# Split first products with one-hot keys from ScalarE in the experts, and GpSimd taking two steps of the picks

## The chip, the cores and the metric

The kernel runs on one NeuronCore of a Trainium2 chip. The metric is the device time of one execution in microseconds. Before the change, three runs gave a median of 3827.49 us (3822.95 to 3830.51). Engines are called TensorE (PE, its weight loads PEld), VectorE (DVE), ScalarE (ACT), GpSimd (POOL) and SyncE (SP, which here only issues DMAs).

## The reference, cut to what matters

Two transformer blocks for 512 tokens of width 1024, in float32. The change touches only the last layer of the second block, a retrieval of single-neuron experts:

```python
def peer(h, w_q, subkeys, u, v):                 # h (512, 1024)
    q = (xc @ w_q).reshape(C, 8, 2, 128)         # 8 heads, 2 halves
    s = einsum('chpd,hpnd->chpn', q, subkeys)    # scores of 2 x 128 keys a head
    sv, si = top_k(s, 16)
    cand    = sv[:, :, 0, :, None] + sv[:, :, 1, None, :]
    cand_id = si[:, :, 0, :, None] * 128 + si[:, :, 1, None, :]
    best, pos = top_k(cand.reshape(C, 8, 256), 16)
    ids = take_along_axis(cand_id.reshape(C, 8, 256), pos)   # 8 x 16 of 16384 experts
    g = softmax(best)
    a = gelu(einsum('cd,chkd->chk', xc, u[ids]))
    return einsum('chk,chkd->cd', g * a, v[ids])
```

## The kernel before, in words

**Picks** (`QueryPicks.run`). For each of 8 heads ScalarE rounds the head's weights (128x2048) to their high part, VectorE subtracts it to get the low part (`lower`, L1884), and TensorE makes 48 products (high x high, high x low, low x high; lines 110 to 112) and 8 score products. ScalarE copies the scores (L1865). VectorE then does the rest of a head: the 16 largest of each half (`top16`), the sums of candidates, the 16 largest of these, the places of the picks in the two lists (`places`), and two look-ups (`look_up`): a one-hot by comparison (L1927), its product with the indices (L1931), and a sum (L1935), each over 128x1024 elements. `keep` and `weigh` store ids and weights. `lower(h + 1)` stands ahead of head h on VectorE.

**Experts** (`peer_experts`). The 512 tokens are dealt with in two ways at once, all engines sharing both:

- The first 256 tokens gather. 512 "rows" (2 tiles of tokens x (u, v) x 128 picks) are fetched by GpSimd with an indirect DMA, 128 lines of 4 KB each (L2075), into a ring of 8 buffers. VectorE uses each in order: for u a product with the tokens and a sum (L2222), for v a multiply and add (L2229). `dealt` fixes how many rows belong to a step: 32 in the lead-in, then 480 over 128 steps, so 3 or 4 a step. A fetch waits until the row 8 earlier is used.
- The last 256 tokens are dense: all 16384 experts in 128 steps of 128. In a step TensorE makes the first products `up` (u tile x tokens, 8 products of 256 columns, L2113), the `gates` of a group of 8 tokens (L2102), and the second products `down` of the step before (L2122). ScalarE takes the GELU (L2169), VectorE multiplies it with the gates to `w` (L2259).
- The gates spread a token's 128 weights over the 16384 experts, a quarter (32 x 128) at a time. For a group, VectorE writes one-hot keys of the second index (`one_hot`, 128x1024, L2184) and of the first (`one_hot_first`, L2196), GpSimd multiplies the latter with the weights' two parts (`weighed`, L2061), TensorE multiplies both, and ScalarE (L2150) and VectorE (L2206) take the result. 32 groups are built in a lead-in ahead of the first step, one more in each of the first 96 steps, none in the last 32.

SyncE loads the u and v tile of each step (0.5 MB each, three buffers of each). The order on each engine is the order of the code; semaphores alone join them. After the experts, `turn` adds the result back into xT, the residual kept in SBUF.

## Time and profile before

| | |
|---|---|
| median of 3 runs | 3827.49 us |
| profiled execution: its time, its span | 3820.54 us, 3818.7 us |
| busy: TensorE, VectorE, ScalarE, GpSimd | 3250.4, 2243.2, 890.2, 996.6 us |
| picks | 2377 to 2627 us |
| lead-in of the experts | 2627 to 2763 us |
| 96 steps with gates | 2763 to 3545 us |
| 32 steps without | 3545 to 3780 us |
| read from HBM | 596.92 MB, over two thirds of it in the experts |

Stages are told from the first and last starts of lines in the trace. Busy times overlap. A matmul's recorded duration is longer than the distance to the next, since they are pipelined: the distance between starts is what one costs. The DMA share is the mean busy share of the 16 queues' engines.

### The profile page before, as it was taken

Reading aid. Unit: us, or ns where it says so; the run is one execution under the profiler, and the core shown is the slowest. Engines: PE = TensorE matmul, PEld = TensorE weight load, DVE = VectorE, ACT = ScalarE, POOL = GpSimd, SP = SyncE. Lnnn points to the kernel's source line nnn. Section 1 sums busy time; section 2 is a strip of 40 time slices with the busy share of each in tenths; the row PEclk is TensorE's granted clock in tenths of the full one; section 3 lists DMA queues with packets and bytes.
Section 4 is the critical chain, followed back from the end, with each engine's and each line's share of the span. In section 5 each row is a group of like instructions: output and inputs, shape, how many; then the busy total and the mean of one; then the engine's idle time right before and its main releaser. Section 6 shows DMA issues by size and latency. Waiting matters only on the chain. (4 is left out here: it accounts for less than half of the span.)

```text
span 3818.7 us, 39393 instructions
## 1 busy us (share of the span) xinstructions
PE 3250.4 (85%) x14052; PEld 2353.1 (62%) x14052; DVE 2243.2 (59%) x3986; ACT 890.2 (23%) x1354; POOL 996.6 (26%) x757
## 2 busy tenths in 40 slices
PE   6779889997968979999498897653599999999997
PEld 4645668875834658878286645443466666666664
DVE  3136433365315643356463434898988999888766
ACT  2133333312214333321324333210100000000001
POOL 0020100000002100000001200003788788888653
PEclk9868999998976989999698878875599999999999
DMA  3320022352330013243134101103499999999996
GB/s 125 132 82 1 28 72 94 108 190 100 136 108 20 1 55 99 94 150 142 63 128 119 31 4 67 51 27 109 141 338 368 373 375 375 367 369 372 401 409 251
DMA packets 206528, 618.01 MB, mean 162 GB/s; under 512 B 31472, under 2 KB 65040, under 8 KB 200720
## 3 DMA queue, kind: packets, MB, share of 16 engines
q1 hardware_dynamic: 132624, 347.28, 25.9%
q0 software_dynamic: 73728, 268.47, 18.9%
q8 instruction: 100, 1.64, 0.2%
q14 instruction: 76, 0.62, 0.1%
HBM read 596.92 MB, written 18.74 MB: 161 GB/s over the span
## 5 line engine op out<-in xcount | busy, mean ns | idle before, releaser
L110 PE MATMUL psum<-sbuf 128*128 128x512 f32 (+1 forms) x1680 | 674.5, 401 | 196.2 <-DVE sbuf L1884 98.9
L111 PE MATMUL psum<-sbuf 128*128 128x512 f32 (+1 forms) x1680 | 660.9, 393 | 0.0
L112 PE MATMUL psum<-sbuf 128*128 128x512 f32 (+1 forms) x1680 | 660.0, 393 | 0.0
L110 PEld LDWEIGHTS psum<-sbuf 128*128 128x128 f32 x1680 | 323.1, 192 | 273.8 <-DVE sbuf L1884 100.8
L2122 PE MATMUL psum<-sbuf 128*128 128x512 f32 x1024 | 469.4, 601 | 5.8 <-DVE sbuf L2259 5.8
L1206 POOL TENSOR_TENSOR sbuf<-sbuf 64x768 fp32r<-64x768 f32 (+2 forms) x22 | 29.2, 1329 | 1689.4 <-ACT sbuf L1152 1689.4
L2113 PE MATMUL psum<-sbuf 128*128 128x256 f32 x2048 | 465.8, 381 | 0.0
L2113 PEld LDWEIGHTS psum<-sbuf 128*128 128x128 f32 x2048 | 391.0, 191 | 107.3 <-issue 60.3
L2075 POOL DMA_INDIRECT sbuf<-peer_u,sbuf x256 | 383.7, 1499 | 96.5 <-issue 55.6
L2075 POOL DMA_INDIRECT sbuf<-peer_v,sbuf x256 | 328.3, 1282 | 154.6 <-DVE sbuf L2229 102.4
L111 PEld LDWEIGHTS psum<-sbuf 128*128 128x128 f32 x1680 | 323.2, 192 | 70.1 <-issue 5.0
L112 PEld LDWEIGHTS psum<-sbuf 128*128 128x128 f32 x1680 | 322.4, 192 | 67.2
L2229 DVE SCALAR_TENSOR_TENSOR sbuf<-sbuf 128x1024 f32<-128x1024 f32 x252 | 313.1, 1281 | 55.8 <-DMA sbuf<-peer_v,sbuf 54.9
L2222 DVE CUSTOM_DVE_ANT_0 sbuf<-sbuf 128x1024 f32<-128x1024 f32 x256 | 326.8, 1322 | 6.6 <-DMA sbuf<-peer_u,sbuf 6.6
L2122 PEld LDWEIGHTS psum<-sbuf 128*128 128x128 f32 x1024 | 186.4, 190 | 195.3 <-issue 183.7
L425 DVE TENSOR_TENSOR sbuf<-sbuf 128x1024 fp32r<-128x1024 f32 x88 | 107.8, 1226 | 298.3 <-ACT sbuf L421 298.3
L2102 PE MATMUL psum<-sbuf 128*128 128x64 f32 x1024 | 166.7, 312 | 92.4 <-DVE sbuf L2184 65.3
L2169 ACT ACTIVATE sbuf<-psum 128x256 f32<-128x256 f32 x128 | 49.1, 383 | 834.0 <-PE psum L2113 834.0
L2102 PEld LDWEIGHTS psum<-sbuf 128*128 128x128 f32 x1024 | 152.6, 225 | 120.7 <-DVE sbuf L2184 80.3
L2184 DVE TENSOR_TENSOR sbuf<-sbuf 128x1024 fp32r<-128x1024 f32 x128 | 195.8, 1529 | 0.0
L964 PE MATMUL psum<-sbuf 128*65 128x512 f32 (+4 forms) x384 | 184.5, 570 | 6.6 <-ACT sbuf L1166 6.3
L1038 DVE TENSOR_REDUCE sbuf<-psum 128x1 f32<-128x128 f32 (+1 forms) x192 | 106.3, 555 | 129.8 <-PE psum L896 82.3
(272 smaller groups left out, 4515.4 us busy)
## 6 DMA issues: line engine op xcount, KB each, us to landing
sbuf<-peer_ut SPq DMA_DIRECT2D x128, 512.0 KB, 8.9
sbuf<-peer_v SPq DMA_DIRECT2D x128, 512.0 KB, 6.7
sbuf<-w_ffn SPq DMA_DIRECT2D x88, 512.0 KB, 3.4
sbuf<-w_mod SPq DMA_DIRECT2D x24, 1024.0 KB, 5.0
sbuf<-w_down SPq DMA_DIRECT2D x16, 1408.0 KB, 6.1
sbuf<-w_fm SPq DMA_DIRECT2D x38, 512.0 KB, 4.4
sbuf<-w_out SPq DMA_DIRECT2D x24, 512.0 KB, 3.5
sbuf<-w_tm SPq DMA_DIRECT2D x10, 1024.0 KB, 5.8
```

What stands on the lines that cost most here:

```text
L110: nc.tensor.matmul(acc, w_high(k), x_high(k), start=(k == 0), stop=False)
L111: nc.tensor.matmul(acc, w_high(k), x_low(k), start=False, stop=False)
L112: mm = nc.tensor.matmul(acc, w_low(k), x_high(k), start=False, stop=(k == kt - 1))
L425: self.nc.vector.tensor_tensor(self.w_low[:, j, :], self.w[:, j, :], self.w_high[:, j, :].bitcast(F32), ALU.subtract).then_inc(self.low_do ...
L964: mm = nc.tensor.matmul(summed[0:W, i % SUMS, x.q0[j]:S], v[0:x.kw[j], x.v, j, :], prob[0:x.kw[j], i % 2, j, x.q0[j]:S], start=(j == 0), s ...
L2075: pool.indirect_dma_start(rows[:, n % RING, :], None, (u, v)[f], bass.IndirectOffsetOnAxis(ap=stream[:, t, j:j + 1], axis=0)).then_inc(gat ...
L2102: mm = nc.tensor.matmul(g_ps[:, n % 2, 2 * j * QUARTER:2 * (j + 1) * QUARTER], hot[:, n % 2, j, :], part[:, n % 2, j, :, :], start=True, s ...
L2113: mm = nc.tensor.matmul(a_ps[:, s % 2, 0:DENSE], u_in[:, s % HELD, k * P:(k + 1) * P], hT[:, k, tok0:S], start=(k == 0), stop=(k == KT - 1))
L2122: mm = nc.tensor.matmul(y_ps[:, 2 * t + half, :], w[:, s % 3, t * P:(t + 1) * P], v_in[:, s % HELD, half * S:(half + 1) * S], start=(s == ...
L2184: nc.vector.tensor_tensor(hot[:, n % 2, :, :], C.iota[:, :].unsqueeze(1).to_broadcast([P, GROUP, NKEY]), picked[:, 1, toks].unsqueeze(2).t ...
L2222: nc.vector.tensor_tensor_reduce(out=rows[:, r, :], in0=rows[:, r, :], in1=h_tok[:, t, :], scale=1.0, scalar=0.0, op0=ALU.mult, op1=ALU.ad ...
L2229: nc.vector.scalar_tensor_tensor(sums, rows[:, r, :], dots[:, t, j:j + 1], sums, ALU.mult, ALU.add).then_inc(used[r], 1)
```

## The change

In `peer_experts`:
- `up` is split in the same three products as the projections (`split_products`), with ScalarE making the high part of each u tile and VectorE the low part, two steps ahead. The tokens' high and low parts are made once, at the start.
- The one-hot keys of the second index go to ScalarE in all groups of the steps and in every other group of the lead-in: (key - index) squared, then ReLU(1 - that).
- To make room, the ring of row buffers lies in xT and hT. xT is stored to HBM at the start of the stage and read back near its end.
- `weighed` runs one group further ahead of the fetches on GpSimd, and u tiles are loaded behind v tiles on SyncE.

In `QueryPicks.run`, GpSimd takes `lower` and the products of the look-ups. `find`, `keep` and `weigh` of a head move into the next head's code.

```diff
@@ picks, VectorE
-                lower(0)
                 for h in range(PH):
-                    if h + 1 < PH:
-                        lower(h + 1)
                     dve.wait_ge(copied, 2 * h + 2)
                     top16([(sc[:, h % 2, p, t, :], sc2[:, p, t, :], val[:, p, t, :], idx[:, p, t, :])
                            for p in range(2) for t in range(ST)])
...
-                    places()
-                    dve.wait_ge(topped, h + 1)
                     if h == 0:
                         dve.wait_ge(iota_landed, 16)
-                    look_up(0)
-                    look_up(1)
-                    keep(h)
-                    if h:
+                    else:
+                        find(h - 1)
+                        keep(h - 1)
                         weigh(h - 1)
+                    places(h)
+                    compare(h)
+                find(PH - 1)
+                keep(PH - 1)
                 weigh(PH - 1)
+
+            @block.gpsimd
+            def _(pool):
+                def lower(h):
+                    pool.wait_ge(high_done, h + 1)
+                    nc.gpsimd.tensor_tensor(w_low[:, h % 2, :], w[:, h % 2, :], w_high[:, h % 2, :].bitcast(F32),
+                                            ALU.subtract).then_inc(low_done, 1)
+
+                lower(0)
+                lower(1)
+                for h in range(PH):
+                    pool.wait_ge(topped, h + 1)
+                    for p in range(2):
+                        n = 2 * h + p
+                        pool.wait_ge(compared, n + 1)
+                        if h:
+                            pool.wait_ge(summed, n - 1)
+                        nc.gpsimd.tensor_tensor(hot2[:, p, :, :].rearrange("p (t k) a -> p t k a", t=ST),
+                                                hot[:, p, :, :].rearrange("p (t k) a -> p t k a", t=ST),
+                                                idf[:, h % 2, p, :, :].unsqueeze(2).to_broadcast([P, ST, T, T]), ALU.mult
+                                                ).then_inc(looked, 1)
+                    if h + 2 < PH:
+                        lower(h + 2)
@@ experts
+    rows = [(xT, hT)[r // 4][:, r % 4 * 2:r % 4 * 2 + 2, :].rearrange("p k s -> p (k s)") for r in range(RING)]
+    def on_act(n):
+        return n >= GROUPS or n % 2 == 1
@@ SyncE
+            sp.dma_start(x_d, xT[:, :, :].rearrange("p k s -> p (k s)")).then_inc(x_stored, 16)
...
+            for n in range(ROWS - RING, ROWS - RING // 2):
+                wait_row(sp, n)
+            sp.dma_start(xT[:, :, :].rearrange("p k s -> p (k s)"), x_d).then_inc(x_back, 16)
@@ GpSimd
                     if n >= RING:
                         wait_row(pool, n - RING)
+                    elif n < RING // 2:
+                        pool.wait_ge(x_stored, 16)
+                    else:
+                        pool.wait_ge(h_low_made, 1)
...
+            weighed(0)
             for step in range(-GROUPS, NKEY):
-                if step + GROUPS < QUARTERS * GROUPS:
-                    weighed(step + GROUPS)
+                if step + GROUPS + 1 < QUARTERS * GROUPS:
+                    weighed(step + GROUPS + 1)
                 fetch_rows(step)
@@ TensorE
-                pe.wait_ge(u_landed[s % HELD], 16 * (s // HELD + 1))
-                for k in range(KT):
-                    mm = nc.tensor.matmul(a_ps[:, s % 2, 0:DENSE], u_in[:, s % HELD, k * P:(k + 1) * P], hT[:, k, tok0:S],
-                                          start=(k == 0), stop=(k == KT - 1))
-                mm.then_inc(a_made, 1)
+                pe.wait_ge(u_low_made, s + 1)
+                split_products(nc, a_ps[:, s % 2, 0:DENSE], KT, lambda k: u_high[:, s % 2, k * P:(k + 1) * P],
+                               lambda k: u_low[:, s % 2, k * P:(k + 1) * P], lambda k: h_high[:, k, :],
+                               lambda k: h_low[:, k, :]).then_inc(a_made, 1)
@@ ScalarE
+            def split_u(s):
+                act.wait_ge(u_landed[s % HELD], 16 * (s // HELD + 1))
+                nc.scalar.activation(u_high[:, s % 2, :], u_in[:, s % HELD, :], ACT.Copy).then_inc(u_high_made, 1)
+            def one_hot(n):
+                if n >= 2:
+                    act.wait_ge(gates_made, n - 1)
+                for j in range(GROUP):
+                    at = n % GROUPS * GROUP + j
+                    nc.scalar.activation(hot[:, n % 2, j, :], C.iota[:, :], ACT.Square, bias=picked[:, 1, at:at + 1],
+                                         scale=-1.0).then_inc(squared, 1)
+                act.wait_ge(squared, GROUP * (squares(n) + 1))
+                nc.scalar.activation(hot[:, n % 2, :, :], hot[:, n % 2, :, :].bitcast(F32), ACT.Relu, bias=C.ones[:, 0:1],
+                                     scale=-1.0).then_inc(one_made, 1)
@@ VectorE
+            def split_u(s):
+                dve.wait_ge(u_high_made, s + 1)
+                if s >= 2:
+                    dve.wait_ge(a_made, s - 1)
+                nc.vector.tensor_tensor(u_low[:, s % 2, :], u_in[:, s % HELD, :], u_high[:, s % 2, :].bitcast(F32),
+                                        ALU.subtract).then_inc(u_low_made, 1)
```

The order of instructions, at three places. First VectorE in the picks, from the places of a head on; before:

```order
L1923 TENSOR_TENSOR sbuf<-sbuf 128x64
L1927 TENSOR_TENSOR sbuf<-sbuf 128x1024
L1931 TENSOR_TENSOR sbuf<-sbuf 128x1024
L1935 TENSOR_REDUCE sbuf<-sbuf 128x64
L1927 TENSOR_TENSOR sbuf<-sbuf 128x1024
L1931 TENSOR_TENSOR sbuf<-sbuf 128x1024
L1935 TENSOR_REDUCE sbuf<-sbuf 128x64
```

The same place now, up to the next head's first search (L1885):

```order
L1919 TENSOR_TENSOR sbuf<-sbuf 128x64
L1927 TENSOR_TENSOR sbuf<-sbuf 128x1024 x2
L1885 MAX sbuf<-sbuf 128x8 x8
L1888 MAX_INDEX sbuf<-sbuf 128x8
L1889 MATCH_REPLACE sbuf<-sbuf 128x128
```

The multiplies left for GpSimd, and the sums come a head later. This is GpSimd's order in the picks now (it had no work there before): L1988 is `lower`, L2000 the two multiplies of a head.

```order
L1988 TENSOR_TENSOR sbuf548<-sbuf533,sbuf547 128x2048 x2
L2000 TENSOR_TENSOR sbuf567<-sbuf566,sbuf555 128x1024 x2
L1988 TENSOR_TENSOR sbuf548<-sbuf533,sbuf547 128x2048
L2000 TENSOR_TENSOR sbuf567<-sbuf566,sbuf555 128x1024 x2
L1988 TENSOR_TENSOR sbuf548<-sbuf533,sbuf547 128x2048
```

The subtract for head h+2 stands behind the multiplies of head h. Last, ScalarE in one dense step with gates, before (L2169 the GELU, L2150 the take of the gates):

```order
L2169 ACTIVATE sbuf<-psum 128x256
L2150 ACTIVATE sbuf<-psum 128x32x8
L2169 ACTIVATE sbuf<-psum 128x256
L2150 ACTIVATE sbuf<-psum 128x32x8
L2169 ACTIVATE sbuf<-psum 128x256
```

and now (L2255 the GELU, L2210 the high part of u, L2229 the take, L2218 and L2221 the one-hot keys):

```order
L2255 ACTIVATE sbuf<-psum 128x256
L2210 ACTIVATE sbuf<-sbuf 128x1024
L2229 ACTIVATE sbuf<-psum 128x32x8
L2218 ACTIVATE sbuf<-sbuf 128x128 x8
L2221 ACTIVATE sbuf<-sbuf 128x1024
```

Ten instructions join the two of a step, and the keys of the next group are written ahead of the next GELU.

## Rows read from the trace of the kernel before

**Rows 1.** Windows by stage: busy time of each engine, clock, DMA share.

```profile
core 0: us, PE busy (x) PEld busy (x) DVE busy (x) ACT busy (x) POOL busy (x), PEclk, DMA share, GB/s
2377.00:2627.00 250.00, 119.93 (x512) 96.87 (x512) 227.09 (x982) 38.55 (x54) 0.00 (x0) 0.74 0.09 30
2627.00:2763.00 136.00, 65.89 (x277) 60.63 (x277) 123.53 (x177) 13.29 (x34) 98.84 (x72) 0.50 0.53 168
2763.00:3545.00 782.00, 758.46 (x3063) 518.45 (x3063) 673.25 (x970) 75.89 (x196) 629.57 (x455) 1.00 0.97 366
3550.00:3750.00 200.00, 195.17 (x674) 127.02 (x672) 136.84 (x130) 11.12 (x29) 115.90 (x102) 1.00 1.03 408
```

**Rows 2.** Waits of VectorE, 2763 to 3545, then 3545 to 3800 (total, times, longest).

```profile
DVE sbuf L2259 <- ACT sbuf L2169: 107.9, 73, 4.6
...
DVE sbuf L2229 <- DMA sbuf<-peer_v,sbuf: 54.9, 63, 1.5
```

**Rows 3.** Timeline of TensorE, one step with gates (start, duration).

```profile
3351.42 3.62 PE L2113 MATMUL psum<-sbuf 128*128 128x256 f32 x16
3354.69 1.16 PE L2102 MATMUL psum<-sbuf 128*128 128x64 f32 x8
3355.68 3.68 PE L2122 MATMUL psum<-sbuf 128*128 128x512 f32 x8
3359.20 0.38 PE L2113 MATMUL psum<-sbuf 128*128 128x256 f32 x1
```

**Rows 4.** Timeline of TensorE, split products of 256 columns in a projection.

```profile
2015.05 0.28 PE L111 MATMUL psum<-sbuf 128*128 128x256 f32 x1
...
2015.89 0.28 PE L112 MATMUL psum<-sbuf 128*128 128x256 f32 x1
```

**Rows 5.** Timeline of the next one-hot; line L2184 in all (minimum, median, maximum).

```profile
3359.36 1.22 POOL L2061 TENSOR_TENSOR sbuf<-sbuf 128x512 fp32r<-128x512 f32 x1
3359.60 2.06 DVE L2184 TENSOR_TENSOR sbuf<-sbuf 128x1024 fp32r<-128x1024 f32 x1
3360.74 1.78 POOL L2075 DMA_INDIRECT sbuf<-peer_u,sbuf  x1 [0.15 <-issue]
3362.82 0.94 POOL L2075 DMA_INDIRECT sbuf<-peer_u,sbuf  x1 [0.30 <-issue]
...
L2184 DVE TENSOR_TENSOR sbuf<-sbuf x128: 1210/1220/2072, 2634.3 to 3539.6; 128x1024 fp32r<-128x1024 f32 x128
```

**Rows 6.** ScalarE lines L2160 and L421 (minimum, median, maximum, ns).

```profile
L2160 ACT ACTIVATE sbuf<-sbuf x2: 309/309/309, 2978.0 to 3532.6; 128x128 f32<-128x128 f32 x2
...
L421 ACT ACTIVATE sbuf<-sbuf x88: 1052/1060/1061, 511.9 to 1663.7; 128x1024 fp32r<-128x1024 f32 x88
```

**Rows 7.** Groups of GpSimd, 2763 to 3545 (busy, mean ns, idle before).

```profile
L2075 POOL DMA_INDIRECT sbuf<-peer_u,sbuf x218 | 322.0, 1477 | 90.0 <-issue 53.0 <-DVE sbuf L2222 35.6 <-DVE sbuf L2229 0.7
L2075 POOL DMA_INDIRECT sbuf<-peer_v,sbuf x141 | 196.3, 1392 | 60.8 <-issue 29.4 <-DVE sbuf L2229 24.3 <-DVE sbuf L2222 5.2
L2061 POOL TENSOR_TENSOR sbuf<-sbuf 128x512 fp32r<-128x512 f32 x96 | 113.9, 1187 | 2.4 <-DVE sbuf L2196 0.8
```

**Rows 8.** Picks: timeline of one head, and group L1931 of 2387 to 2600.

```profile
2451.86 1.23 DVE L1927 TENSOR_TENSOR sbuf<-sbuf 128x1024 f32<-128x1024 f32 x1
...
2460.29 2.28 DVE L1884 TENSOR_TENSOR sbuf<-sbuf 128x2048 fp32r<-128x2048 f32 x1
...
2479.29 1.09 ACT L1865 ACTIVATE sbuf<-psum 128x512 f32<-128x512 f32 x2 [2.14 <-PE psum L1835]
2479.95 1.22 DVE L1927 TENSOR_TENSOR sbuf<-sbuf 128x1024 f32<-128x1024 f32 x1
...
L1931 DVE TENSOR_TENSOR sbuf<-sbuf 128x1024 f32<-128x1024 f32 x14 | 17.2, 1226 | 0.5
```

**Rows 9.** Groups, 2637 to 2763 (the lead-in).

```profile
L2222 DVE CUSTOM_DVE_ANT_0 sbuf<-sbuf 128x1024 f32<-128x1024 f32 x32 | 64.1, 2004 | 6.6 <-DMA sbuf<-peer_u,sbuf 6.6
L2075 POOL DMA_INDIRECT sbuf<-peer_u,sbuf x38 | 61.7, 1623 | 6.6 <-issue 2.6
```

**Rows 10.** Timeline of the end of the experts.

```profile
3775.16 0.42 DVE L2259 TENSOR_TENSOR sbuf<-sbuf 128x256 f32<-128x256 f32 x1
...
3782.95 8.20 PE L1754 MATMUL psum<-sbuf 128*128 128x128 f32 x32 [3.61 <-PEq L2015]
```

More of the change, by code:

```diff
@@ L1803, in run @@
                                        "topped", "was_shifted", "exp_done", "did_step")]
+            compared, looked, summed = [sem.one(x) for x in ("compared", "looked_up", "found_summed")]
             block = ctx.enter_context(nc.Block())
@@ L1938, in keep, with find @@
+                def find(h):
+                    for p in range(2):
+                        dve.wait_ge(looked, 2 * h + p + 1)
+                        nc.vector.tensor_reduce(found[:, p, :], hot2[:, p, :, :], AX_X, ALU.add).then_inc(summed, 1)
+                    dve.wait_ge(summed, 2 * h + 2)
                 def keep(h):
@@ L1987, with peer_experts @@
 GROUP = 8
-def peer_experts(nc, C, hT, h_tok, stream, ids, weights, ut, u, v, u_in, y):
+def peer_experts(nc, C, xT, hT, h_tok, stream, ids, weights, ut, u, v, u_in, y, x_d):
     DENSE = (ST - GT) * P
@@ L2009, in dealt, with squares @@
         return EARLY + (ROWS - EARLY) * (step + 1) // NKEY
+    def on_act(n):
+        return n >= GROUPS or n % 2 == 1
+    def squares(n):
+        return sum(map(on_act, range(n)))
     def row(n):
@@ L2043, in _, with load_u @@
         def _(sp):
+            def load_u(s):
+                if s >= HELD:
+                    sp.wait_ge(u_low_made, s - HELD + 1)
+                sp.dma_start(u_in[:, s % HELD, :], ut[s]).then_inc(u_landed[s % HELD], 16)
+            sp.dma_start(x_d, xT[:, :, :].rearrange("p k s -> p (k s)")).then_inc(x_stored, 16)
+            for s in range(HELD):
+                load_u(s)
             for s in range(NKEY):
-                if s >= HELD:
-                    sp.wait_ge(a_made, s - HELD + 1)
-                sp.dma_start(u_in[:, s % HELD, :], ut[s]).then_inc(u_landed[s % HELD], 16)
                 if s >= HELD:
@@ L2096, in gates @@
             def gates(n):
-                pe.wait_ge(hot_made, n + 1)
+                if on_act(n):
+                    pe.wait_ge(one_made, squares(n) + 1)
+                else:
+                    pe.wait_ge(own_made, n - squares(n) + 1)
                 pe.wait_ge(parts_made, n + 1)
@@ L2221, in use_row @@
                 if f == 0:
-                    nc.vector.tensor_tensor_reduce(out=rows[:, r, :], in0=rows[:, r, :], in1=h_tok[:, t, :], scale=1.0,
+                    nc.vector.tensor_tensor_reduce(out=rows[r], in0=rows[r], in1=h_tok[:, t, :], scale=1.0,
                                                    scalar=0.0, op0=ALU.mult, op1=ALU.add,
```

89 lines of the change are left out of this document (57 added, 32 removed).

## The prediction

> **What bounds the kernel now.** Read the windows by stage first [rows 1]. Four stages matter. In the picks (2377 to 2627 us) VectorE is busy 227 of 250 us and GpSimd not at all. In the lead-in of the experts (to 2763) VectorE is busy 123.5 of 136 us at the low clock level of TensorE (0.50). In the first 96 dense steps (2763 to 3545, 782 us or 8.15 us a step) TensorE is busy 97%, with the DMA queues at 366 GB/s. In the last 32 steps, which have no gates to build, the queues move 408 GB/s.
>
> Then the waits [rows 2]. In the 96 steps VectorE never waits for a gathered row, only for ScalarE's GELU, which means for TensorE. In the last 32 steps it waits 54.9 us for rows. So the 96 steps are bound by TensorE, and the last 32 by transfers.
>
> The timeline of one step [rows 3] shows what TensorE does in 7.78 us (3351.42 to 3359.20): 3.27 us to the gates, 1.0 us of gates, 3.5 us of second products. The mean of 8.15 is 0.37 us more; I put it down to gates that wait for VectorE's one-hot keys.
>
> **The first products of the experts.** Eight 4-byte products of 256 columns, two passes each (16 records), become 24 single-pass products. The trace has just that shape: the split products of 256 columns in the projections start 0.12 us apart (seven intervals from 2015.05 to 2015.89 [rows 4]). 24 x 0.12 = 2.88 us for 3.27 us, so 0.39 us less. The one-hot wait of 0.37 us goes too, since ScalarE makes the keys ahead. TensorE would allow 7.39 us a step.
>
> **What the others allow.** VectorE loses the one-hot of 128x1024 (L2184) and gains the low part of u, the same shape and the same two inputs in SBUF: a swap. Its busy time stays 673/96 = 7.0 us a step. It may be blocked the same way as now: beside GpSimd's multiply the one-hot took 2.06 us for 1.22 [rows 5].
>
> ScalarE gains, per step, eight squares of 128x128 (0.31 us each as the GELU of that size, 2.5 in all), a ReLU and a copy of 128x1024 (1.06 each), beside its two present operations of 0.38: 5.4 us [rows 6]. Two ends for the squares: 0.2 and 0.5 us, so 4.5 to 6.9. All are under 7.4, and the keys are needed only after the next first products, so I cost this at nothing. If the cover went, the gates would wait on ScalarE.
>
> GpSimd keeps its work, in another order. Per step it is busy 629.6/96 = 6.56 us, and waits another (53.0 + 29.4)/96 = 0.86 us for nothing but its own issue [rows 7]: 7.42 us. This is the term that I think ends last. A gather's issue takes 0.94 us at the least and 1.78 beside a VectorE instruction [rows 5]; the mean over 359 was 1.44. As steps shorten, VectorE's busy share grows from 0.86 to 0.92, and with it the part of issues that pay the 0.84 us: 0.06 x 0.84 x 3.75 = 0.2. So 7.65 us a step.
>
> DMA: a step moves two tiles and 3.75 gathered rows of 0.524 MB, 3.015 MB. At the 408 GB/s of the last stage that is 7.39 us.
>
> The Trainium skill (DMA: Bandwidth & Descriptors, Specifications) states a limit of about 358 GB/s of HBM for a core, with 368 as the vendor's derated figure. By that rule the 366 GB/s of the 96 steps would already be the limit, and the faster products would give nothing there. This trace disagrees: 408 GB/s for 200 us in the next stage. I go by the row, and keep the rule's outcome as a rival.
>
> I take 7.65 us: 96 x (8.15 - 7.65) = 48 us off. Bounds: 7.39 (73 us off) and 8.15 (nothing).
>
> The last 32 steps: TensorE gets faster, but transfers bound them. VectorE, busy 136.8 of 200 us or 5.0 us of a step of 235/32 = 7.3, gains 1.2: 6.2, still inside. Zero; ends are 5 us less and 5 us more.
>
> **The picks.** A head takes 28.1 us, compare to compare (2451.86 to 2479.95 [rows 8]), all of it VectorE. It loses the subtract of 128x2048 (2.28) and two multiplies of 128x1024 (1.23 each, with their gaps 1.26): 28.1 - 2.2 - 2.5 = 23.4 us.
>
> But the low part of the weights for head h+2 now stands on GpSimd behind head h's two multiplies. The trace has no GpSimd operation so large. From its 128x512 at 1.19 us [rows 7] I estimate 2.4 us a multiply and 4.8 us for the subtract, some 9.6 us after the second compare. Queued behind is everything for head h+2: in the row before, from the end of the subtract (2462.57) to the copied scores (2480.38) went 17.8 us, partly at the low clock level. So scores come 9.6 + 17.8 = 27.4 us after the compare of two heads earlier, while VectorE needs 23.4 a head. It waits every other head: two heads take 27.4 + 23.4, or 25.4 each. Seven heads save 7 x 2.7 = 19 us. The first head pays 2.5 us more for its subtract, and the last lays bare the multiplies, about 3 us. Net 14 us off. Bounds: 30 us off, if GpSimd's operations run at half my estimate; 10 us more, if VectorE is blocked behind each. I am near the first since the 10 us beside them are MAX8 and FIND_INDEX8, with one large input.
>
> The Trainium skill (GPSIMD Engine Reference, § 3.1) has 4497 ns for a GpSimd add of 2048 elements a partition against 2293 on VectorE. The trace agrees on VectorE's side (2.28); no row shows GpSimd's, and by its figure the 4.8 would be 4.5.
>
> **The lead-in.** 32 groups last about 3.75 us each, 120 us (VectorE's 123.5 less some 3.5 ahead of the first), with a row's product blocked to 2.0 us [rows 9]. VectorE keeps every other one-hot (1.2 us), so a group needs 3.2 us of it on average; GpSimd needs 1.1 + 1.6 + 0.4 = 3.1, and ScalarE about the same. I take 3.3: 15 us off. Against it: two subtracts of u (2.4 us), and the first gather, which now waits for 2.1 MB to be stored, 5 us at 408 GB/s and some latency, while the first row already waited 6.6 us [rows 9]. That adds 6. Net 6 off (20 off to 10 more).
>
> **The end.** xT is read back after rows 504 to 507. These are used in step 126, before the last weights at 3775.16, so the 2.1 MB (5.1 us and 2 of latency) land by 3782.5; the next block began at 3782.95 [rows 10]. 1.5 us more; bounds 0 and 6.
>
> **Sum.** -48 -14 -6 +1.5 = -66.5 us from the profiled execution's 3820.5: 3754. The median of the runs is 7 us above that execution, so 3761.
>
> **Rivals.**
> - *Everything reaches the floor of transfers.* GpSimd's issues fit their gaps, and the 96 steps run at 7.39 us (73 off), the picks and the lead-in take 30 off instead of 20. For it: the gaps between GpSimd's issues may shrink where none follows a wait. Against: all engines would have to run without a gap. 3827.5 - 103 + 2 = 3726. Chance 0.15.
> - *Transfers bind already at 366 GB/s.* The 96 steps give nothing, the rest 20: 3808. For it: the DMA share is 0.97 there. Against: no wait for a row in 782 us, and 408 GB/s later. Chance 0.08.
> - *The change doesn't do what it says:* the first products are no faster, as each brings a weight load, busy 518.45 us / 3063 = 0.17 us by [rows 1]: 24 x 0.17 = 4.1 us. The 0.12 us between starts in [rows 4] speaks against, since loads stood there too. TensorE would need 7.39 - 2.88 + 4.1 = 8.6 us a step, 0.45 x 96 = 43 us more, and 20 less elsewhere: 3850. Chance 0.01.
> - *Slower: GpSimd is locked out.* If VectorE, now without pauses, stands in front of every gather, each takes 1.78 + 0.30 us, and a step 1.34 + 3.75 x 2.08 = 9.1 us: 96 x 1 us more, less 20 elsewhere, so about 3900. It decides once the mean issue passes 1.57 us (a step of 8.37), from 1.44 now. Against: in the last stage most issues were free. Chance 0.05.
> - *Forecast*: 0.71, own range 3735 to 3785.
>
> The range must leave out 2 in 10: 3722 to 3808. A difference under 0.2% (7.7 us) cannot be told from none. Faster by more: 0.91, within: 0.03, slower: 0.06.
>
> **What would show it.** First products of 24 records in 2.9 us; a step of 7.6 us in the 96, near 395 GB/s, with GpSimd's issue gaps but hardly a wait for VectorE; in the picks alternate heads with a VectorE wait of about 4 us for the copied scores, and GpSimd operations of 2.4 and 4.8 us; lead-in groups alternating about 3.8 and 2.8 us; the last stage unchanged at 408 GB/s with waits for rows. I would be wrong in the main term if the step stays at 8 us or more with GpSimd or ScalarE named as what the others wait for.

## The result, and the profile after

| | before | after |
|---|---|---|
| median | 3822.95 us (3821.99 to 3830.51, 5 runs) | 3766.9 us (3763.24 to 3795.65, 5 runs) |
| ratio, 95% interval | | 0.9864 (0.9831 to 0.9896) |

The change makes the kernel 1.4% faster, 52 us by the interval's middle and 56 by the medians. Forecast were 3761 us, a saving of 66.5 from the 3827.49 measured before. In a second measurement, beside the variants below, the same kernel took 3770.9 us for 3813.66 (0.9879, 0.9861 to 0.9898), 46 us less.

The profiled execution of the first measurement is its slowest (3795.65 us): the first copy of picked indices (L1964) starts at 2438.0 us, in another profiled execution of the same kernel (span 3772.6) at 2417.1, as in the kernel before (2416.8). The code ahead of the picks is unchanged; its length differs by 21 us between these two executions and by 32 us over all the profiles below (the first search starts between 2395.8 and 2428.1), so I compare stages, not spans. The views below are of the second execution unless another is named.

Windows by stage (busy time and count of each engine, granted clock, DMA share, GB/s), in the order of [rows 1]:

```profile
2377.00:2605.00 228.00, 119.85 (x512) 96.82 (x512) 185.75 (x955) 37.30 (x52) 79.89 (x24) 0.77 0.10 33
2605.00:2744.00 139.00, 68.25 (x308) 65.05 (x308) 116.09 (x164) 77.55 (x192) 99.18 (x72) 0.50 0.59 188
2744.00:3506.00 762.00, 718.71 (x3831) 518.30 (x3831) 712.19 (x970) 490.00 (x1148) 643.50 (x456) 0.97 0.99 378
3511.00:3711.00 200.00, 184.22 (x888) 124.40 (x887) 166.78 (x156) 37.21 (x56) 126.39 (x102) 0.97 1.03 409
```

The picks have given up some 22 us, the 96 steps 19. TensorE has 43 us idle in the 96 steps (24 before) and for the first time a granted clock below 1 there. VectorE is busy 712 us where it was 673, though it was to be a swap. The stages measured from the first and last starts of the same lines in each trace:

| us | before | after | keys on ScalarE, float32 products (f32_up) | forecast |
|---|---|---|---|---|
| picks, a head | 27.7 | 24.0 | 24.0 | 25.4 |
| end of the picks to the experts | 21.3 | 24.6 | 24.6 | +3 |
| to the first GELU (lead-in) | 137.9 | 134.9 | 125.0 | -6 |
| 96 steps | 780.6 | 761.4 | 749.1 | -48 |
| of these a step in the u, v, u stretch | 8.14, 8.07, 8.21 | 7.97, 7.44, 8.21 | 7.67, 7.79, 7.86 | 7.65 |
| last 31 steps | 221.4 | 220.6 | 221.4 | 0 |
| from the last GELU to the end | 46.8 | 46.4 | 49.4 | +1.5 |

(A "u stretch" has steps in which VectorE uses u rows: the GELUs of steps 0 to 25 and 60 to 94; in 26 to 60 they are v rows. The picks are counted from copy to copy of L1964, whose first interval is short, 19.7 us in the kernel after. The step between the first u stretch and the v stretch stands outside the three: 12.3 us after, 7.8 before.)

Waits in the 96 steps (engine, line, releaser: us in total, times, longest), against [rows 2]:

```profile
ACT sbuf L2255 <- PE psum L112: 216.1, 86, 5.2
...
PE psum L2164 <- issue: 30.7, 37, 2.4
DVE sbuf L2312 <- DMA sbuf<-peer_u,sbuf: 27.7, 42, 2.4
...
DVE sbuf L2360 <- ACT sbuf L2255: 18.4, 8, 3.8
```

VectorE's wait for the GELU fell from 107.9 to 18.4 us: it is hardly TensorE any more that it waits for. New is that VectorE waits 42 times for a gathered u row. And TensorE stands longer ahead of the gates (L2164): 30.7 us here and 12.4 more for ScalarE's keys, where it was 23.0 us in all before (14.2 without a named releaser, 8.8 for VectorE's keys).

An undisturbed step of TensorE, of the first profiled execution (start, duration, engine, line), against [rows 3]:

```profile
2990.14 0.68 PE L110 MATMUL psum<-sbuf 128*128 128x256 f32 x1
...
2990.78 0.28 PE L112 MATMUL psum<-sbuf 128*128 128x256 f32 x1
2990.90 0.28 PE L110 MATMUL psum<-sbuf 128*128 128x256 f32 x1
2991.02 0.28 PE L111 MATMUL psum<-sbuf 128*128 128x256 f32 x1
...
2993.42 0.98 PE L2164 MATMUL psum<-sbuf 128*128 128x64 f32 x8
2994.23 3.68 PE L2184 MATMUL psum<-sbuf 128*128 128x512 f32 x8
2997.34 0.68 PE L110 MATMUL psum<-sbuf 128*128 128x256 f32 x1
```

From the second on the split products start 0.12 us apart, as in [rows 4], and the whole step takes 7.20 us (2990.14 to 2997.34), 0.58 less than before. Only the distance from one step to the next tells this: from the first product's recorded start to the gates it is 3.28 us, 3.27 before, but that start lies 0.5 us ahead of the second's, among the last of the second products. 24 x 0.12 = 2.88 us, then 0.81 to the second products (0.99 before), leave 3.51 for those, as before (3.52). TensorE has this speed to give. A step in a u stretch takes 8.0 to 8.2 all the same. What such a step looks like, the same execution, all engines, TensorE's first products left out:

```profile
3254.70 0.38 ACT L2255 ACTIVATE sbuf<-psum 128x256 f32<-128x256 f32 x1 [2.46 <-PE psum L112]
3254.86 0.08 DVE L2312 DVE_READ_ACCUMULATOR2_ANT sbuf<- 128x1 f32 x1
3254.86 1.21 DVE L2312 CUSTOM_DVE_ANT_0 sbuf<-sbuf 128x1024 f32<-128x1024 f32 x1
3254.98 1.05 ACT L2210 ACTIVATE sbuf<-sbuf 128x1024 fp32r<-128x1024 f32 x1
3255.75 1.23 POOL L2115 TENSOR_TENSOR sbuf<-sbuf 128x512 fp32r<-128x512 f32 x1
...
3257.08 1.05 PE L2164 MATMUL psum<-sbuf 128*128 128x64 f32 x8 [2.42 <-issue]
3257.13 0.98 POOL L2133 DMA_INDIRECT sbuf<-peer_u,sbuf  x1 [0.15 <-issue]
3257.48 1.23 DVE L2312 CUSTOM_DVE_ANT_0 sbuf<-sbuf 128x1024 f32<-128x1024 f32 x1 [1.41 <-DMA sbuf<-peer_u,sbuf]
```

TensorE stands still for 2.42 us. The profile names no releaser, but the gates start 0.1 us after the end of GpSimd's multiply of the weights (3255.75 + 1.23 = 3256.98), which gives them their moving side; the other two things that the code has them wait for, the keys and the space in PSUM, were ready by 3252.3. The multiply itself waited for nothing: it follows directly on a fetch that began at 3253.76 and took 1.98 us. VectorE then waits 1.41 us for a row. So GpSimd holds both.

GpSimd's own account, two stretches of 200 us (busy, mean ns, idle before). First 3250 to 3450, u rows, 25 steps; then 3000 to 3200, v rows, 27 steps:

```profile
L2133 POOL DMA_INDIRECT sbuf<-peer_u,sbuf x95 | 145.9, 1536 | 25.0 <-issue 19.1 <-DVE sbuf L2286 4.9
L2115 POOL TENSOR_TENSOR sbuf<-sbuf 128x512 fp32r<-128x512 f32 x26 | 30.6, 1177 | 0.4
```

```profile
L2133 POOL DMA_INDIRECT sbuf<-peer_v,sbuf x101 | 117.7, 1165 | 26.6 <-issue 24.8
L2115 POOL TENSOR_TENSOR sbuf<-sbuf 128x512 fp32r<-128x512 f32 x27 | 51.0, 1887 | 6.4 <-DVE sbuf L2286 4.9 <-issue 1.5
```

With u rows 145.9 + 30.6 + 25.4 = 201.9 us fill the 200, 4.9 us of them a wait for VectorE. Per step: 3.8 fetches of 1.536 + 0.263 us and a multiply of 1.2, 8.0 us. With v rows a fetch costs 1.165 and the multiply 1.887, and GpSimd waits 4.9 us for VectorE's first keys (L2286). In [rows 7] the means were 1.477 and 1.392 for a fetch.

In the v stretch another engine ends last. VectorE there, and the window:

```profile
L2319 DVE SCALAR_TENSOR_TENSOR sbuf<-sbuf 128x1024 f32<-128x1024 f32 x101 | 145.9, 1501 | 0.0
L2334 DVE TENSOR_TENSOR sbuf<-sbuf 128x1024 fp32r<-128x1024 f32 x27 | 32.7, 1212 | 0.0
...
3000.00:3200.00 200.00, 197.09 (x1085) 143.70 (x1085) 199.91 (x209) 138.29 (x324) 167.13 (x128) 1.00 1.02 407
```

VectorE is busy 199.9 of 200 us and waits for nothing; the stretch runs at VectorE's 7.44 us a step, with the queues at 407 GB/s.

ScalarE in the 96 steps, against [rows 6]:

```profile
L2218 ACT ACTIVATE sbuf<-sbuf 128x128 fp32r<-128x128 f32 x760 | 231.5, 393 | 0.0
L2221 ACT ACTIVATE sbuf<-sbuf 128x1024 fp32r<-128x1024 f32 x95 | 109.4, 1152 | 3.1
L2210 ACT ACTIVATE sbuf<-sbuf 128x1024 fp32r<-128x1024 f32 x97 | 101.7, 1048 | 0.0
```

A square is recorded with 393 ns, but eight take 2.44 us (231.5/95): 5.4 us a step with the rest, as forecast (5.1 with the overlaps of neighbours counted once, 490.0/96). The Trainium skill (ScalarE: Activation LUTs, *What ACT_TABLE_LOAD costs*) has 280 ns + 0.833 ns an element for an ACTIVATE with a pointer bias, 387 ns here, and back-to-back ones overlapping by some 93 ns; the rows agree.

The picks, against [rows 8], timeline of GpSimd and then of VectorE:

```profile
2448.98 5.52 POOL L2000 TENSOR_TENSOR sbuf<-sbuf 128x1024 f32<-128x1024 f32 x2 [13.02 <-DVE sbuf L1927]
2454.47 4.50 POOL L1988 TENSOR_TENSOR sbuf<-sbuf 128x2048 fp32r<-128x2048 f32 x1
...
2447.62 2.36 DVE L1927 TENSOR_TENSOR sbuf<-sbuf 128x1024 f32<-128x1024 f32 x2
2452.49 1.65 DVE L1885 MAX8 sbuf<-sbuf 128x8 f32<-128x128 f32 x8 [2.51 <-ACT sbuf L1866]
```

Two multiplies and the subtract take 10.0 us (I had 9.6), and every other head VectorE waits 2.1 to 3.3 us for the copied scores, here 2.51; at the heads between it is 0.3 to 0.7. The subtract's 4.50 us is the 4.497 that the Trainium skill gives for GpSimd (GPSIMD Engine Reference, § 3.1).

The end, against [rows 10]:

```profile
3738.60 8.20 PE L1754 MATMUL psum<-sbuf 128*128 128x128 f32 x32 [5.01 <-PEq L2052]
```

The transposes wait 5.01 us for the last code of the experts, not 3.61. What that code waits for is xT, which SyncE asked for at 3729.59 and which lands 8.6 us later, 0.4 us ahead of the transposes:

```profile
SPq L2052 <- DMA sbuf<-x_kept: 8.2, 1, 8.2
```

### The profile page after: what moved, and what is told of

Same layout as the page of the kernel before. It is cut to its first block and busy times, and to the rows that moved or that the text cites. A ratio compares the mean times of both kernels' runs of the same rounds, so it can differ in the third digit from the quotient of the medians.

```text
span 3793.8 us, 42758 instructions
## 1 busy us (share of the span) xinstructions
PE 3215.9 (85%) x15076; PEld 2359.0 (62%) x15076; DVE 2260.5 (60%) x3979; ACT 1396.2 (37%) x2491; POOL 1103.1 (29%) x781
## 5 line engine op out<-in xcount | busy, mean ns | idle before, releaser
L110 PE MATMUL psum<-sbuf 128*128 128x512 f32 (+1 forms) x2704 | 1016.1, 376 | 182.8 <-POOL sbuf L1988 84.2
L111 PE MATMUL psum<-sbuf 128*128 128x512 f32 (+1 forms) x2704 | 951.8, 352 | 0.0
L112 PE MATMUL psum<-sbuf 128*128 128x512 f32 (+1 forms) x2704 | 950.6, 352 | 0.0
L110 PEld LDWEIGHTS psum<-sbuf 128*128 128x128 f32 x2704 | 520.0, 192 | 290.4 <-POOL sbuf L1988 86.2
L111 PEld LDWEIGHTS psum<-sbuf 128*128 128x128 f32 x2704 | 520.1, 192 | 100.6 <-issue 35.2
L112 PEld LDWEIGHTS psum<-sbuf 128*128 128x128 f32 x2704 | 519.2, 192 | 67.8
L2184 PE MATMUL psum<-sbuf 128*128 128x512 f32 x1024 | 494.6, 628 | 16.7 <-DVE sbuf L2360 16.7
L2133 POOL DMA_INDIRECT sbuf<-peer_u,sbuf x256 | 396.8, 1550 | 64.4 <-issue 44.1
L2312 DVE CUSTOM_DVE_ANT_0 sbuf<-sbuf 128x1024 f32<-128x1024 f32 x256 | 378.7, 1508 | 32.7 <-DMA sbuf<-peer_u,sbuf 32.0
L2319 DVE SCALAR_TENSOR_TENSOR sbuf<-sbuf 128x1024 f32<-128x1024 f32 x252 | 339.8, 1386 | 33.7 <-DMA sbuf<-peer_v,sbuf 33.7
L2184 PEld LDWEIGHTS psum<-sbuf 128*128 128x128 f32 x1024 | 193.8, 199 | 219.6 <-issue 199.2
L425 DVE TENSOR_TENSOR sbuf<-sbuf 128x1024 fp32r<-128x1024 f32 x88 | 107.9, 1226 | 297.3 <-ACT sbuf L421 297.3
L2218 ACT ACTIVATE sbuf<-sbuf 128x128 fp32r<-128x128 f32 x896 | 272.9, 392 | 0.0
L2164 PE MATMUL psum<-sbuf 128*128 128x64 f32 x1024 | 158.2, 307 | 110.4 <-DVE sbuf L2274 52.6
L2164 PEld LDWEIGHTS psum<-sbuf 128*128 128x128 f32 x1024 | 152.2, 230 | 121.0 <-DVE sbuf L2274 63.2
L1179 ACT ACTIVATE sbuf<-psum 128x512 f32<-128x512 f32 (+1 forms) x240 | 122.2, 510 | 261.7 <-PE psum L928 125.7
L2255 ACT ACTIVATE sbuf<-psum 128x256 f32<-128x256 f32 x128 | 49.1, 384 | 414.5 <-PE psum L112 414.5
L421 ACT ACTIVATE sbuf<-sbuf 128x1024 fp32r<-128x1024 f32 x88 | 93.3, 1060 | 292.9 <-PE psum L112 292.5
```

What stands on the lines that cost most here:

```text
L110: nc.tensor.matmul(acc, w_high(k), x_high(k), start=(k == 0), stop=False)
L111: nc.tensor.matmul(acc, w_high(k), x_low(k), start=False, stop=False)
L112: mm = nc.tensor.matmul(acc, w_low(k), x_high(k), start=False, stop=(k == kt - 1))
L425: self.nc.vector.tensor_tensor(self.w_low[:, j, :], self.w[:, j, :], self.w_high[:, j, :].bitcast(F32), ALU.subtract).then_inc(self.low_do ...
L1179: nc.scalar.activation(prob[0:x.kw[j], i % 2, j, x.q0[j]:S], shifted[0:x.kw[j], (block0[i] + j) % 2, x.q0[j]:S], ACT.Exp, scale=HD ** -0.5 ...
L2133: pool.indirect_dma_start(rows[n % RING], None, (u, v)[f], bass.IndirectOffsetOnAxis(ap=stream[:, t, j:j + 1], axis=0)).then_inc(gathered[ ...
```

## The experiments

Each was measured in five rounds beside the kernel before. Ratios are to it, with 95% intervals. "After again" is the unchanged kernel after. The first four shared one chip, the next four a second, the last three a third.

| | median, us | ratio |
|---|---|---|
| after_again | 3770.9 | 0.9879 (0.9861 to 0.9898) |
| picks_only | 3794.15 | 0.9949 (0.9931 to 0.9967) |
| experts_only | 3795.48 | 0.9945 (0.9929 to 0.9962) |
| f32_up | 3756.3 | 0.9842 (0.9826 to 0.9858) |
| no_low | 3737.68 | 0.9799 (0.9779 to 0.9818) |
| rows_by_sp | 3732.87 | 0.9788 (0.9775 to 0.9802) |
| keys_first | 3757.73 | 0.9859 (0.984 to 0.9878) |
| f32_orders | 3742.12 | 0.9805 (0.9791 to 0.9818) |
| keys_on_dve | 3915.12 | 1.0277 (1.025 to 1.0303) |
| f32_weighed_late | 3767.77 | 0.9874 (0.9858 to 0.9891) |
| both_orders | 3754.95 | 0.9839 (0.9824 to 0.9854) |

**The whole again, and each half alone** (after_again, picks_only: `peer_experts` of before; experts_only: `QueryPicks.run` of before).

> The changed kernel once more, for a second profile. The first one was 29 us longer than the median of its runs, and some 15 us of that lay ahead of the picks. Both theories: a median near 3767 us, and a profile that reaches the picks 10 to 15 us sooner. In the 96 steps with gates, theory GpSimd (its fetches and multiply end last while u rows are gathered) expects 7.2 us a step while v rows are gathered and about 8 while u rows are; theory transfers (the queues' rate ends last) expects about the same step in both, since the bytes are the same.

> The kernel before with the changed picks alone. By the trace of the changed kernel a pair of heads takes 49.4 us for 56.2, and the two ends give some back: 15 to 22 us less than before, so 3802 to 3808 us. If the experts had gained from it in another way (a later clock rise), it would be under 10 us.

> The changed kernel with the picks of before. The rest of the change: 56 us less in all, less the picks' 15 to 22, so 34 to 41 us less than before, 3782 to 3789 us.

picks_only wins 0.51% (19.5 us), experts_only 0.55% (21 us), together 40.5 of the whole's 46; the intervals allow a plain sum. For picks_only that was expected; for experts_only 34 to 41 us were, because the expectation took 56 us for the whole and gave the experts all that the picks left. The halves stand apart in the stages too: experts_only has the old 27.7 us a head, picks_only the old 780.5 us for the 96 steps. after_again bears out the theory of GpSimd in its direction, with unequal steps in u and v stretches (7.97 and 7.44); its 7.2 us in the v stretch isn't reached, since VectorE ends last there.

**The split products taken out** (f32_up). ScalarE's keys, the ring's place and GpSimd's order stay. With the products go both halves of the split of u and VectorE's low part of the tokens.

```diff
-                pe.wait_ge(u_low_made, s + 1)
-                split_products(nc, a_ps[:, s % 2, 0:DENSE], KT, lambda k: u_high[:, s % 2, k * P:(k + 1) * P],
-                ...
+                pe.wait_ge(u_landed[s % HELD], 16 * (s // HELD + 1))
+                for k in range(KT):
+                    mm = nc.tensor.matmul(a_ps[:, s % 2, 0:DENSE], u_in[:, s % HELD, k * P:(k + 1) * P], h_kept[:, k, :],
+                                          start=(k == 0), stop=(k == KT - 1))
```

> The changed kernel with the first products of the experts in float32 in two passes again, as before; the keys stay on ScalarE, the high and low parts of u and of the tokens are left out (one copy of the tokens stays). TensorE then needs 7.78 us a step with gates and 6.89 without. Theory GpSimd: VectorE loses 1.2 us a step, so blocks GpSimd less; the 96 steps run at 7.8 to 7.9 us, about as long as the changed kernel's mean of 7.9, and the total is within 15 us of it. Theory products (the shorter products made the gain): 7.78 plus the waits of the changed kernel, about 8.3 us a step, 35 us more than the changed kernel.

It is 0.37% faster than the kernel after on the same chip, 14.6 us, as the theory of GpSimd had it. Its 96 steps:

```profile
2740.00:3489.00 749.00, 744.16 (x3058) 520.84 (x3057) 604.27 (x874) 403.69 (x1047) 618.99 (x457) 1.00 1.00 386
```

TensorE is busy 744 of 749 us with the clock at 1.00 throughout: this kernel is at the 7.78 us of [rows 3] and hardly anything holds it up. Its GpSimd, 3250 to 3450:

```profile
L2132 POOL DMA_INDIRECT sbuf<-peer_u,sbuf x97 | 134.0, 1381 | 25.6 <-issue 24.7 <-DVE sbuf L2285 0.6
L2114 POOL TENSOR_TENSOR sbuf<-sbuf 128x512 fp32r<-128x512 f32 x26 | 37.9, 1457 | 3.6 <-DVE sbuf L2285 2.1 <-issue 1.0
```

A fetch takes 1.38 us where it takes 1.54 in the kernel after. VectorE has one 1.2 us instruction less in a step; f32_up alone can't tell this from the rest that was taken out, no_low does.

**Only VectorE's subtract of u taken out** (no_low). ScalarE's copy and the 24 products stay; TensorE and the loads of the next u tile wait for the copy instead.

```diff
-                               lambda k: u_low[:, s % 2, k * P:(k + 1) * P], lambda k: h_high[:, k, :],
+                               lambda k: u_high[:, s % 2, k * P:(k + 1) * P], lambda k: h_high[:, k, :],
...
-                nc.vector.tensor_tensor(u_low[:, s % 2, :], u_in[:, s % HELD, :], u_high[:, s % 2, :].bitcast(F32),
-                                        ALU.subtract).then_inc(u_low_made, 1)
+                return
```

> The changed kernel without VectorE's subtract of u: the low part is left out, and the third product takes the high part in its place, so TensorE does the same 24 products. Theory GpSimd: the subtract (1.2 us a step) is what VectorE blocks GpSimd and itself with in the stretches where u rows are gathered; without it the issue of a fetch falls from 1.55 us to about 1.35 as in the kernel with float32 products, these stretches from 8.1 to about 7.5 us a step, and the total by about 35 us to some 3735. Theory clock and transfers: the step stays above 7.9 there, and the total falls by less than 12 us.

0.0080 of the time, 31 us, hangs on that one instruction and on what waited for it (two jobs, each beside its own kernel before). The expectation was 35 us. The 96 steps fall to 733.4 us (7.64 a step, u stretches 7.41 and 7.72), the lead-in to 125.3. The mean fetch of u rows, 2710 to 3460, is 1.346 us; in the 96 steps of the kernel after it was 1.542. ScalarE does here all that it does in the kernel after, so ScalarE is not what binds.

```profile
L2133 POOL DMA_INDIRECT sbuf<-peer_u,sbuf x222 | 298.8, 1346 | 59.4 <-issue 45.3 <-DVE sbuf L2286 11.3
```

**GpSimd relieved of the fetches** (rows_by_sp). SyncE loads the rows as plain blocks of the same size.

```diff
+                    sp.dma_start(rows[n % RING], (u, v)[f][j * P:(j + 1) * P, :]).then_inc(gathered[n % RING], 16)
...
-                fetch_rows(step)
```

> The changed kernel with the 512 row fetches issued by SyncE as plain loads of 128 consecutive rows (the same bytes, not the rows that were picked, so the result is another), none by GpSimd, which keeps its multiplies. Theory GpSimd: its term is gone and all stretches run at TensorE's 7.2 or the transfers' 7.4 us a step, some 50 us less in the 96 steps; total near 3720. Theory transfers: no change in the 96 steps, within 12 us of the changed kernel.

The lowest median of all, with an interval that overlaps no_low's: the 96 steps take 724.1 us, 7.54 a step, though VectorE still has the subtract. That is 37 us less in the 96 steps, where 50 had been expected. Windows inside the u, v and u stretches:

```profile
2760.00:2950.00 190.00, 184.05 (x1005) 134.38 (x1005) 180.32 (x283) 130.44 (x303) 41.86 (x25) 0.99 1.01 400
2970.00:3200.00 230.00, 226.11 (x1251) 165.73 (x1249) 229.72 (x246) 161.38 (x373) 58.83 (x31) 1.00 1.02 406
3220.00:3450.00 230.00, 221.46 (x1205) 161.45 (x1203) 219.08 (x350) 158.57 (x367) 50.57 (x31) 0.99 1.02 404
```

The same bytes go through at 400 to 406 GB/s, where the kernel after had 378 over the stage and 380 in the second u stretch. So transfers do not bind the kernel after in its u stretches. Taking out either the subtract or the fetches gains 28 and 37 us in the 96 steps, most of it in the u stretches, which fits that there it is the pair that costs. In the v stretch it is not: the step stays at 7.40 us for 7.44, and VectorE is busy 229.7 of 230 us. A kernel with neither wasn't run, so what the subtract still costs without the fetches isn't shown.

**Orders** (keys_first, f32_orders, both_orders). keys_first writes ScalarE's keys ahead of the GELU's wait. f32_orders is f32_up with that, and with GpSimd's subtract in the picks ahead of the look-ups' multiplies; both_orders is the kernel after with the same two.

```diff
+            one_hot(GROUPS)
...
-                if s + GROUPS < QUARTERS * GROUPS and on_act(s + GROUPS):
-                    one_hot(s + GROUPS)
...
+                if s + GROUPS + 1 < QUARTERS * GROUPS:
+                    one_hot(s + GROUPS + 1)
```

```diff
@@ picks, GpSimd, ahead of the multiplies of head h
+                    if h + 2 < PH:
+                        lower(h + 2)
...
-                    if h + 2 < PH:
-                        lower(h + 2)
```

> The changed kernel with ScalarE writing the next group's keys ahead of the GELU of the dots, which waits for the last u row of a tile. That wait stands ahead of the keys in two steps of 128, where TensorE then stood 5 us and ran its next second products at the low clock level (6.6 us for 3.7). If both are due to the order: 2 x 8 = 16 us less than the changed kernel at most, about 10 expected, since the gathers behind lose less. If the stall comes from the missing rows themselves, nothing (under 4 us).

> The kernel with float32 first products (15 us under the changed kernel) and two orders changed: the keys ahead of the GELU of the dots, and in the picks GpSimd making the low part for head h+2 before the multiplies of head h, not behind them. The second frees a head from the wait for its scores: 24.0 us a head fall to VectorE's 23.4 or less, and the first scores of a pair come sooner; 5 us less in the picks. With 3 to 5 us for the keys: 3746 to 3750 us. If VectorE is blocked by the 4.5 us subtract instead, a head stays at 24 us or gets longer.

> The kernel after (split first products) with both changes of order that f32_orders has: ScalarE's keys ahead of the GELU, and GpSimd's subtract of the weights ahead of the look-ups' multiplies. Theory: the split products still cost 10 us in the lead-in and about nothing in the 96 steps once ScalarE's keys are early (745.9 us of keys_first against 744.2 of f32_orders), so 3750 to 3756 us, some 10 us over the 3742 of f32_orders. Rival: the orders take away all that the split products cost, and it is at or under f32_orders, 3735 to 3743 us.

keys_first gives 0.20% over the kernel after, from two jobs (intervals that overlap), so it is likely and not settled; its 96 steps took 745.9 us for 761.4, half of the gain at the two changes from u to v rows (12.3 to 8.9 us for the step at the first, 17.5 to 13.1 for the last two), and its last 31 steps 224.6 for 220.6. In the picks the order gives 1.4 us a head (22.53 for 23.96): VectorE's waits for copied scores fall from 33.6 us to the 24.1 of the first head.

```profile
DVE sbuf L1885 <- ACT sbuf L1866: 33.6, 7, 24.1
```

```profile
DVE sbuf L1885 <- ACT sbuf L1866: 24.1, 1, 24.1
```

(The kernel after, then f32_orders.) f32_orders beats both kernels, by 1.95% over before, and by more than was expected (3742 for 3746 to 3750), since the picks gave 10 us and not 5. both_orders against it is the second estimate of what the split products cost: 0.9839 against 0.9805, 13 us (first: 14.6), where some 10 were expected. By stages 10.6 us of that are the lead-in (134.8 and 124.2) and the 96 steps are about equal (742.0 and 744.2).

**Keys back on VectorE** (keys_on_dve), with the split products kept:

```diff
     def on_act(n):
-        return n >= GROUPS or n % 2 == 1
+        return False
```

> The kernel after with all one-hot keys back on VectorE; the split first products and the rest stay. Theory: the gain in the experts comes from the keys' move, and the split products alone cost time, since VectorE then has both the keys (1.2 us) and the subtract of u (1.2 us) in a step. In the 96 steps of the kernel after VectorE was busy 706.9 us of 761; 96 keys more make 824 us, 8.6 us a step, and more where GpSimd's multiply blocks them, so 8.6 to 9.0 a step, 60 to 100 us more than the kernel after; with 16 keys more in the lead-in, where VectorE has no pauses, 10 to 15 us more. In all 3840 to 3885 us, slower than before by 1 to 2%. Rival: the keys' move gives nothing and the split products gave the 19 us of the 96 steps; then 3765 to 3785 us, faster than before.

The direction is the theory's, the size is not: 2.8% slower than before (1 to 2% expected), 9.20 us a step. In the 96 steps (groups of VectorE, then a wait of TensorE):

```profile
L2333 DVE TENSOR_TENSOR sbuf<-sbuf 128x1024 fp32r<-128x1024 f32 x96 | 147.9, 1540 | 7.5 <-ACT sbuf L2210 6.4 <-issue 1.1
L2273 DVE TENSOR_TENSOR sbuf<-sbuf 128x1024 fp32r<-128x1024 f32 x95 | 115.4, 1215 | 0.0
```

```profile
PE psum L2164 <- DVE sbuf L2273: 107.1, 59, 4.4
```

VectorE is busy 822 us, 8.6 a step, as worked out, yet the stage lasts 884. TensorE waits 107 us for the keys, and VectorE then waits 49 us for the GELU behind TensorE: the engines take turns instead of running beside each other. TensorE's granted clock also falls to 0.92 in this stage, from 0.97. The expectation priced only the busy time.

**GpSimd's multiply in its old place** (f32_weighed_late), float32 products:

```diff
-            weighed(0)
...
-                if step + GROUPS + 1 < QUARTERS * GROUPS:
-                    weighed(step + GROUPS + 1)
+                if step + GROUPS < QUARTERS * GROUPS:
+                    weighed(step + GROUPS)
```

> The kernel with float32 first products and ScalarE's keys, but GpSimd multiplies the keys with the weights in the old place, for the group at hand and not one ahead. Theory: the 8.15 us of a step before were 7.78 us of TensorE and a wait of the gates; f32_up took all of that wait away (7.80 us a step). If the multiply that stands one group ahead is what took it away, the steps go back to 7.9 to 8.15 us here, 3770 to 3790 us in all. Rival: ScalarE's early keys alone took it away, and this kernel equals f32_up within 5 us, 3752 to 3762 us.

Between the two theories: 7.87 us a step, where f32_up has 7.80 and before 8.13. So ScalarE's early keys took 25 us off the 96 steps, and the multiply's place 7 (and 2.6 in the lead-in). The ratios of the two kernels are 0.32% apart, from two jobs, with intervals that just touch.

A kernel that splits the first products in the v stretch alone, where they gain (7.79 to 7.44 us a step), would need the tokens in both forms in SBUF, and wasn't tried. By the stages I estimate it at 34 x 0.35 = 12 us.

## Why the prediction was right, point by point

The total was right (3761 for 3766.9, within the range) with a wrong inner split. The 96 steps gave 19 us where I had 48, the picks 22.6 where I had 14, the lead-in 3 for 6. The two errors partly cancel, which is luck, and the kernel before came out 4.5 us below the median that I had counted from, which brings the time closer than the saving: 66.5 us were forecast, 46 to 56 measured.

1. **First products, 0.39 us less a step; the key wait of 0.37 goes.** TensorE's own step is 7.20 us, less than my 7.39 by what lies between the start of the gates and that of the second products (0.81 for 0.99 us). The wait for the keys can go: f32_up has 7.80, TensorE's 7.78. In the kernel after other waits stand in its place, 43 us for GpSimd's multiply and for ScalarE's keys together.
2. **VectorE, "a swap".** This step failed. The count and shape were right, but I kept its busy time at 673 us. Its row products now take 1.42 us for a u row and 1.48 for a v row (311.0 us for 224, 188.0 for 132), where they took 1.23 and 1.28, since GpSimd's multiply meets them; before, it met the keys, which took 2.06 us beside it [rows 5]. rows_by_sp has 1.39 and 1.47 without any fetch, so it is the multiply. At 712 us VectorE is busy 7.4 us a step and not 7.0, and in the v stretch it is what ends last: 199.9 of 200 us, 7.44 a step. no_low shows the price of the subtract in the whole: without it 31 us less.
3. **GpSimd's issues, "the term that ends last".** The right term for the u stretches, mis-sized, and not the last one with v rows. I raised the mean fetch by 0.05 us, from 1.44; with u rows it became 1.54, with v rows 1.17, and over the stage it fell to 1.41 (336.2 + 171.3 us for 361). The multiply, which I left at 1.19 us, takes 1.44 on average. So u stretches stay at 8.0 to 8.2 us, the v stretch reaches 7.44 (forecast 7.65 for all). 96 steps gave 19 us, not 48.
   My own sign of being wrong, a step of 8 us or more with GpSimd named as what the others wait for, is met in the second u stretch (8.21) and nearly in the first (7.97); the mean of the 96 steps is 7.93.
   The rival "GpSimd is locked out" was to decide from a mean of 1.57 and a step of 8.37. The u stretches come within 0.03 us of that mean, but with v rows GpSimd is freer than before, and the rival's 9.1 us a step is nowhere near.
   The Trainium skill (SBUF — State Buffer, *Who interferes with whom*) says that a VectorE instruction with two SBUF inputs contends with a GpSimd instruction that reads SBUF. Whether a fetch's issue counts as one it doesn't say; the same section infers that such a VectorE instruction leaves the making of descriptors for GpSimd's transfers alone. no_low speaks against that inference: 1.35 us a fetch without the subtract for 1.54 with it.
4. **ScalarE at 5.4 us, hidden.** The duration is right, the cover mostly. Twice the keys come much too late, when ScalarE waits for the last u row of a tile of tokens (first profiled execution):

```profile
2971.31 0.31 ACT L2239 ACTIVATE sbuf<-sbuf 128x128 f32<-128x128 f32 x1 [6.96 <-DVE sbuf L2312]
...
2973.99 1.15 ACT L2221 ACTIVATE sbuf<-sbuf 128x1024 fp32r<-128x1024 f32 x1
...
2975.18 1.92 PE L2164 MATMUL psum<-sbuf 128*128 128x64 f32 x8 [4.88 <-ACT sbuf L2221]
...
2976.91 6.60 PE L2184 MATMUL psum<-sbuf 128*128 128x512 f32 x8
```

   The keys stand behind that GELU in ScalarE's order, so TensorE waits 4.88 us; and after the stall its second products, at the low clock level, take 6.60 us and not 3.68. keys_first writes them ahead.
5. **Transfers, 408 GB/s.** They didn't bind the u stretches: those move 380 GB/s, and rows_by_sp 400 to 404 in the same place. In the v stretch the kernel after moves 407 GB/s, nearly the 409 of its last stage, so there they are close to binding too, though VectorE never waits for a row. The last 31 steps are unchanged, as forecast. The rivals of a limit at 366 GB/s and of all at the transfer floor both fall, the first by 378 to 389 GB/s in the 96 steps (the kernel after, f32_up, keys_first, no_low), the second by the u stretches.
6. **Picks, 14 us off.** 22.6 us in the traces (7 x 3.7, less 3.3 at the end), 19.5 by picks_only. GpSimd's prices were right (10.0 us for 9.6), but the first multiply starts before the second compare has ended, and the scores follow the subtract in 16.5 to 17.9 us, where I took 17.8 from a stretch partly at the low clock. Alternate heads take 25.2 to 26.3 us and 23.4 to 23.8; 27.4 and 23.4 were forecast.
7. **Lead-in, 6 us off.** 3 us by the traces. f32_up's is 10 us shorter (125.0), and so is no_low's, which only lacks VectorE's subtracts of u (125.3). I had priced two subtracts at 2.4 us; they also wait for ScalarE's copies, in the kernel after (2612 to 2744):

```profile
DVE sbuf L2334 <- ACT sbuf L2210: 5.9, 2, 3.0
```

   With 2.5 us for the two that is 8.4 of the 10. GpSimd's fetches don't tell the difference here (1.65 us after, 1.62 in no_low). rows_by_sp comes to 125.0 in another way: its subtracts wait as long (6.7 us), but VectorE's row products take 63.0 us for 69.7 and the first row comes 3 us sooner.
8. **The end, +1.5.** The wait grew by 1.4 us (5.01 for 3.61); the tail as a whole is equal within 0.4. Between the kernels of the table above it differs by up to 6 us (44.1 in rows_by_sp, 50.2 in no_low), which was not looked into.

In one sentence: the gain is the picks (20 us) and the keys' move with GpSimd's order (some 38 us, f32_up against picks_only); the split first products, which I had counted on in the largest term of my sum, cost 13 to 15 us as they stand. Their low part is made on VectorE, where it lengthens GpSimd's fetches in the u stretches, fills VectorE in the v stretch, and waits for ScalarE in the lead-in.

## What to carry to other kernels

Before an engine's work is swapped for other work of the same length, look at what shares a resource with it: here the new 1.2 us on VectorE were as long as the old, and GpSimd's multiply and fetches met other instructions than before. Price an issuing engine by stretch, with the mean of its issues in the stretch with the tightest pattern, not over a stage. A faster product is worth only what the engine that feeds it has left over, so make the feed first, on an engine with room, and then split.
